# Expert 0 and overflow blocks in a leading loop, fifteen experts written out behind it, and the tables of two later layers built beside the second layer's output product

## The reference

```python
ang = positions[..., None] * inv_freq            # rope tables, same for both layers
cos, sin = jnp.cos(ang), jnp.sin(ang)
for l in range(2):
    q, k, v, cb, cc, cu, qm, gates = split(x @ w_in[l])
    q, k = rope(q, cos, sin), rope(k, cos, sin)
    lam = exp(sum(lq1[l] * lk1[l])) - exp(sum(lq2[l] * lk2[l])) + lam_init
    y_attn = diff_attention(q, k, v, lam, lam_init, g)
    y_mem = memory_attention_2(qm, mem, w_mem_kv[l])   # needs mem turned to columns
    x = layer_norm(ALPHA * x + merge(y_attn, conv, y_mem) @ w_out[l])
    x = layer_norm(ALPHA * x + grouped_moe(x, w_router, bias, w_gate[l], w_up[l], w_down[l]))
```

## Time and profile before

| | |
|---|---|
| median of 3 runs | 3729.55 us (3728.22 to 3733.88) |
| the profiled execution, its own time | 3737.84 us |
| its span in the trace | 3736.2 us |
| PE busy | 3048.7 us, 82% |
| DVE busy | 1926.2 us, 52% |
| ACT busy | 1078.1 us, 29% |
| DMA | 467.63 MB, mean 125 GB/s |
| mean granted TensorE clock | 0.889 of full |

### The profile page before, as it was taken

One profiled execution on the slowest core, in us unless ns is written; L12 is line 12 of the kernel. 1 busy time (PEld: TensorE's weight loads), 2 busy tenths in 40 slices (PEclk: granted clock), 3 DMA queues, 4 the chain that ended last, 5 costly groups with the idle time before them and its releaser, 6 DMA issues. The chain is left out here.

```text
span 3736.2 us, 35502 instructions
## 1 busy us (share of the span) xinstructions
PE 3048.7 (82%) x13366; PEld 2421.3 (65%) x13366; DVE 1926.2 (52%) x2791; ACT 1078.1 (29%) x1837; POOL 308.2 (8%) x472
## 2 busy tenths in 40 slices
PE   4969978798898498989985699749898998569973
PEld 3758856677776376766875477637676687457762
DVE  3562344351664444655543587644465454358754
ACT  2341130210441102151001477510215100147742
POOL 0020030000440001210000000010121000000001
PEclk8989999788899698979997799969997999779996
DMA  2212202122601131202323599623120222369973
GB/s 86 79 57 90 90 28 82 37 90 81 263 1 57 59 97 57 78 5 71 99 79 148 221 374 363 229 96 102 61 75 5 79 91 79 148 230 373 371 264 112
DMA packets 151663, 467.63 MB, mean 125 GB/s; under 512 B 15022, under 2 KB 29256, under 8 KB 126152
## 3 DMA queue, kind: packets, MB, share of 16 engines
q1 hardware_dynamic: 142136, 431.31, 32.6%
q0 software_dynamic: 9360, 34.08, 2.3%
HBM read 413.46 MB, written 51.90 MB: 125 GB/s over the span
## 5 line engine op out<-in xcount | busy, mean ns | idle before, releaser
L154 DVE CAST weights_r<-weights 128x1024 fp32r<-128x1024 f32 (+4 forms) x270 | 229.1, 848 | 845.1 <-DMA weights<-in_w_in 314.6
L147 PE MATMUL ps<-x_cols_hi_r,weights_r 128*128 128x512 f32 x896 | 361.9, 404 | 49.4 <-DVE weights_r L156 49.4
L156 DVE TENSOR_TENSOR weights_r<-weights,weights_r 128x1024 fp32r<-128x1024 f32 (+4 forms) x270 | 385.8, 1429 | 9.3
L148 PE MATMUL ps<-x_cols_lo_r,weights_r 128*128 128x512 f32 x896 | 357.9, 399 | 0.0
L149 PE MATMUL ps<-x_cols_hi_r,weights_r 128*128 128x512 f32 x896 | 357.9, 399 | 0.0
L147 PEld LDWEIGHTS ps<-x_cols_hi_r,weights_r 128*128 128x128 f32 x896 | 171.7, 192 | 95.6 <-DVE weights_r L156 54.1
L943 POOL TENSOR_SCALAR weights<-weights,weight 128x256 f32<-128x256 f32 (+3 forms) x304 | 152.5, 522 | 778.4 <-DVE weight L837 467.5
L887 ACT ACTIVATE weights<-weights,minus_top 128x256 f32<-128x256 f32 (+3 forms) x304 | 167.0, 551 | 147.3 <-DVE minus_top L800 147.3
L148 PEld LDWEIGHTS ps<-x_cols_lo_r,weights_r 128*128 128x128 f32 x896 | 171.6, 192 | 41.6 <-issue 1.4
L149 PEld LDWEIGHTS ps<-x_cols_hi_r,weights_r 128*128 128x128 f32 x896 | 171.3, 191 | 40.8
L147 PE MATMUL ps<-hawk_xT_hi_r,weights_r 128*128 128x512 f32 x384 | 155.5, 405 | 25.5 <-DVE weights_r L156 25.5
(11 more groups left out here) (466 smaller groups left out, 6947.2 us busy)
## 6 DMA issues: line engine op xcount, KB each, us to landing
weights<-in_w_in SPq DMA_DIRECT2D x64, 1024.0 KB, 5.3
raw_pieces<-in_w_exp_down SPq DMA_DIRECT2D x46, 1024.0 KB, 7.5
raw_pieces<-in_w_exp_up SPq DMA_DIRECT2D x36, 1024.0 KB, 7.1
weights<-in_w_exp_gate SPq DMA_DIRECT2D x34, 1024.0 KB, 6.1
raw_pieces<-in_w_exp_gate SPq DMA_DIRECT2D x32, 1024.0 KB, 6.3
weights<-in_w_exp_up SPq DMA_DIRECT2D x30, 1024.0 KB, 7.4
weights<-in_hawk_w_in SPq DMA_DIRECT2D x28, 1024.0 KB, 5.3
weights<-in_w_exp_down SPq DMA_DIRECT2D x20, 1024.0 KB, 8.0
```

What stands on the lines that cost most here:

```text
L147: pe.matmul(out, as_r(left[1]), as_r(right[0]), start=start, stop=False)
L148: pe.matmul(out, as_r(left[0]), as_r(right[1]), start=False, stop=False)
L154: dve.tensor_copy(as_r(hi), lo).then_inc(rounded, 1)
L156: dve.tensor_tensor(as_r(lo), lo, as_r(hi).bitcast(F32), ALU.subtract).then_inc(done, 1)
```

## The change

It has four parts.

1. `rope_tables`, `diff_lambda`, the rotation load and the turning of the second layers' memory are gone as stages. A "rider" (`tables_rider`) does their work inside the NSA output product: SP issues its twelve loads ahead of the weights, PE transposes the memory rows after steps 0 and 1 (into banks 4 to 7, which the left half does not use), ACT rounds them and does exponentials and sines, DVE works after the weight splits of steps 1 to 4. The results lie in tensors of the whole program; the attention memory tensors of the first layers use the same space.
2. `final_norm` is one stage, and norm and gain are one DVE pass.
3. In `experts` the loop stands first. Its iteration 0 is expert 0, the others are the overflow blocks; in each, SP loads the next block's x and pieces as the present block's are used, and DVE splits the down pieces ahead of `hidden`. After the last iteration the same rooms hold expert 1. Experts 1 to 15 are then written out. `route` computes the row slots for that order, with two more small loads and four more small DVE operations at its end.
4. In the written-out part the second up piece is rounded and split behind the hidden rows, not ahead of them.

The core of the diff (what is left out is the same code under new names, and the angle arithmetic, which is unchanged):

```diff
+    rider = rider or bag(names=(), sync=None, pe={}, dve={}, act=None)
+    with Tensors(nc) as sb, stage(nc, "weights_loaded*2", "rounded", "y_split", "weights_split", "read", *rider.names) as (block, s):
...
+            if rider.sync:
+                rider.sync(sp, s)
...
+                if q in rider.pe:
+                    rider.pe[q](pe, s)
...
                 if q == per_half:
                     add(0)
+                if q in rider.dve:
+                    rider.dve[q](dve, s)
...
+    def sync(sp, s):
+        sp.dma_start(rows[:, :, :], a["mem_2"][0].rearrange("(t p) d -> p t d", p=P)).then_inc(s.mem_loaded, 16)
+        sp.dma_start(pos[:, :], a["positions_2"].partition_broadcast(P)).then_inc(s.tables_loaded, 16)
+        sp.dma_start(freq[:, :], a["rope_freq"]).then_inc(s.tables_loaded, 16)
+        for i, name in enumerate(("q1", "q2", "k1", "k2")):
+            for layer in range(2):
+                sp.dma_start(lam[:, i, layer, :], a[f"lambda_{name}_2"][layer:layer + 1, :].partition_broadcast(P)).then_inc(s.tables_loaded, 16)
+        sp.dma_start(m.late.rotate[:, :], a["rotate"]).then_inc(s.tables_loaded, 16)
...
+    def turn(ks):
+        def run(pe, s):
+            pe.wait_ge(s.mem_loaded, 16)
+            for k in ks:
+                if k >= 4:
+                    pe.wait_ge(s.mem_split, k - 3)
+                for t in range(MT):
+                    mm = pe.transpose(m.ps[:, bank_of(k) + t * P:bank_of(k) + (t + 1) * P], rows[:, t, k * P:(k + 1) * P], m.ident[:, :])
+                mm.then_inc(s.mem_turned, 1)
...
+    def mem_low(ks):
+        def run(dve, s):
+            for k in ks:
+                dve.wait_ge(s.mem_taken, k + 1)
+                dve.tensor_tensor(as_r(memT.lo[:, k, :]), m.ps[:, bank_of(k):bank_of(k) + N_MEM], as_r(memT.hi[:, k, :]).bitcast(F32),
+                                  ALU.subtract).then_inc(s.mem_split, 1)
...
+    def lambdas(dve, s):
+        dve.wait_ge(s.tables_loaded, 16 * 11)
...
+               sync=sync, act=act, pe={0: turn(range(4)), 1: turn(range(4, DK)), 2: banks_free},
+               dve={1: both(mem_low(range(4)), lambdas), 2: mem_low(range(4, DK)), 3: angle(sin, 0.0),
+                    4: both(angle(cos, 0.25), finish_lambdas)})
...
+            for i in range(2):
+                sp.dma_start(own[:, i, :], a["own_block"][i:i + 1, :].partition_broadcast(P)).then_inc(s.loaded, 16)
...
+def ring_plan():
+    order = [(1, p) for p in GATE]
+    for b in range(1, N_EXPERTS):
         order += [(b, p) for p in UP]
...
+    room = {(1, p): p for p in range(6)}
+    room.update({(2, p): 6 + p for p in GATE + UP})
+    held = [job for job in order if job in room]
+    after = {}
+    for job in order:
+        if job not in room:
+            before = held.pop(0)
+            room[job], after[job] = room[before], order.index(before)
+            held.append(job)
...
+    for b, rooms in ((0, range(6)), (2, range(6, RAW_ROOMS))):
+        for room in rooms:
+            p = room % 6
+            sp.dma_start(as_loaded(raw[room], p), expert_piece(a, layer, b, p)).then_inc(m.expert_fetched, 16)
...
+            with sp.Fori(0, late) as i:
+                expert = sp.value_load(moe.late_expert[0:1, bass.ds(i, 1)], min_val=0, max_val=LAST)
+                row = sp.value_load(moe.late_row[0:1, bass.ds(i, 1)], min_val=0, max_val=MAX_BLOCKS - 1)
+                sp.wait_ge(s.first_x_turned, 2 * i + 2)
+                sp.dma_start(xe[:, :], rows_at(moe.x_rows, row)).then_inc(s.first_x_loaded, 16)
+                for p in range(6):
+                    sp.wait_ge(s.first_used, 6 * i + (7 + p))
+                    sp.dma_start(as_loaded(raw[p], p), expert_piece(a, layer, expert, p)).then_inc(s.first_loaded[p], 16)
...
+                sp.wait_ge(s.first_loaded[p], 16 * late + 16)
+                sp.sem_inc(s.loaded[p], 16)
...
+            with pe.Fori(0, late) as i:
+                pe.wait_ge(s.first_x_split, 2 * i + 2)
+                for p in GATE + UP:
+                    pe.wait_ge(s.first_split, 6 * i + (p + 1))
+                    project(xT[0], p, p, gate_bank if p in GATE else up_bank, s.first_used)
+                pe.wait_ge(s.first_x_loaded, 16 * i + 32)
+                turn_x(s.first_x_turned)
+                pe.wait_ge(s.first_hidden_done, i + 1)
+                turn_h(s.first_h_turned)
+                pe.wait_ge(s.first_h_split, i + 1)
+                pe.wait_ge(s.first_out_taken, 2 * i + 2)
+                for p in DOWN:
...
+                first_round(GATE + UP)
+                act.wait_ge(s.first_used, 6 * i + 8)
+                silu(s.first_silu_done)
+                first_round(DOWN)
+                act.wait_ge(s.first_used, 6 * i + 10)
+                act.wait_ge(s.first_h_turned, i + 1)
+                round_h(s.first_h_rounded)
+                round_x(xT[0], s.first_x_turned, 2 * i + 2, s.first_x_rounded)
+                act.wait_ge(s.first_used, 6 * i + 12)
+                act.wait_ge(s.first_y_left, i + 1)
+                take_out(s.first_out_taken)
...
+                if b > 1:
+                    static_take_out(b - 1)
+                if b < LAST:
+                    static_round_x(b + 1)
+                round_pieces(b, DOWN)
+                if b < LAST:
+                    round_pieces(b + 1, UP[:1])
...
+                if b < LAST:
+                    round_pieces(b + 1, UP[1:])
...
+                for p in GATE + UP + DOWN:
+                    dve.wait_ge(s.first_rounded, 6 * i + (p + 1))
+                    split_piece(p, p, s.first_split)
+                dve.wait_ge(s.first_silu_done, i + 1)
+                dve.wait_ge(s.first_used, 6 * i + 10)
+                hidden(s.first_hidden_done)
+                dve.wait_ge(s.first_h_rounded, i + 1)
+                split_h(s.first_h_split)
+                split_x(xT[0], s.first_x_rounded, 2 * i + 2, s.first_x_split)
...
+            for t in range(TT):
+                dve.scalar_tensor_tensor(out=x[:, t, :], in0=x[:, t, :], scalar=inv[:, t:t + 1], in1=g[:, :], op0=ALU.mult, op1=ALU.mult)
...
-        with stage(nc, "loaded") as (block, s):
-            @block.sync
-            def _(sp):
-                sp.dma_start(m.rotate[:, :], a["rotate"]).then_inc(s.loaded, 16)
-                sp.wait_ge(s.loaded, 16)
-        rope_tables(nc, m, a, cos, sin)
-        normed_memory(nc, m, a["mem_2"][0], None, memT)
```

646 lines of the change are left out of this document (319 added, 327 removed).

## The result

The changed kernel takes **3627.91 us** (median of 4 runs, 3617.87 to 3633.0) against 3728.89 for the kernel before (4 runs), a ratio of 0.9723 with a 95% interval of 0.9699 to 0.9747: 101 us less. The forecast was 3645.0 with a range from 3632 to 3670.

The account below looks back on a forecast made before the run. Bound: chain length between NSA product and next layer, PE in the product, PE with its wait in written-out blocks, DMA just behind. Terms summed to -84.6 us: 3737.84 to 3653.2, less 8.3 for the median, 3645.0; range 3632 to 3670.

Parts of the forecast that it names:

- Stages that go: Stages removed between NSA product and next layer (-31.5 and -0.9) and two lambda stages (-15.2); together -47.6 us.
- What the product takes on: NSA output product: 16 more PE transposes cost +2.1 us, DVE's added work fits its gaps; ends 1.5 and 14.
- 0 to 2: NSA output product: SP issues twelve loads ahead of the first weights' signal, costing 0 to 2 us.
- C: NSA output product: PE waits for DVE in steps 2 to 5; +14 instead of +2.1, 3656.9 us; chance 0.06.
- The loop: Expert loop: x rounding -1.0, table load +1.3, down wait -1.7, clock -1.5; -2.9 us each, three times -8.7.
- -8.7 - 2.8 + 1.2 + 1.6: Loop iterations, ramp into the written-out part, loop-count reads, and two more small router loads per layer, in us.
- The written-out blocks: Written-out experts: PE's hidden_T_lo wait goes, mean period 19.87 to 18.7 us, 26 times: -30.4; ends -15.6 and -38.
- rival B: Written-out blocks: HBM gives no more than 370 GB/s, the wait moves to a load; gain 0, 3675.4 us; chance 0.12.
- reserve: Written-out blocks: some 7.5 us of loads ahead, dry after 8.6 blocks at 18.4 us, then 19.27 us each.
- A: Written-out blocks: DMA binds from the first one, 19.27 us each; term -15.6, 3659.8 us; chance 0.20.
- E: Written-out blocks: ring never runs dry, 18.4 us throughout; term -38.2, 3637.2 us; chance 0.57 together with the forecast.
- D: Written-out blocks: lower clock makes down 2.7 us longer per block; +70, 3745.6 us; chance 0.02.

Follow-up runs that it names:

- e3: Changed kernel with `route` and `experts` of the kernel before, so only parts 1 and 2 are made; 3694.6 us (0.9900).
- e7_small: Changed kernel with four small costs taken out: rider loads issued later, own_block loads not awaited by PE, loop count read later, ACT's loop begun at silu; 3628.71 us.
- e5: Kernel before with part 3 alone, both up pieces still ahead of hidden_T_lo; 3732.02 us (1.0005).
- e2: Changed kernel with part 4 undone, both up pieces again rounded and split ahead of hidden_T_lo; 3677.71 us.
- e1: Kernel before with part 4 alone; 3683.04 us (0.9872).
- e4: Changed kernel with one of three matmul passes left out of the down product in the written-out blocks; 3586.1 us.
- e10: Changed kernel with one more 1 MB load, read by nobody, for each of blocks 2 to 14 of the written-out part; 3662.94 us.
- e9: e7_small with DVE following ACT's roundings of block 1 piece by piece, not waiting for all four; 3621.97 us (0.9709).
- e12: e9 with ACT rounding the next block's two gate pieces ahead of the outputs in the loop, and DVE splitting them there; 3598.32 us (0.9646).

## Why the prediction was right or wrong

**Stages that go: right.** Forecast -32.4 between product and next layer, measured -32.6 (44.76 to 12.18). PE starts 14.6 us behind the last add of the product, "some 15" in the forecast. The lambda stages: forecast -15.2; the stretch from projection to mask is 15.5 shorter in e3 and 18.4 in after, measured on the profiled execution of before. About 15 of it are the two stages (7.6 and 7.4 us in before); the rest is the scatter of the projection.

**What the product takes on: right mechanism, 1.5 short.** Forecast +2.1, measured +3.65. The transposes are 2.05 of it (PE's first 72 matmuls take 20.48 us with them, 18.43 without). 1.3 of the rest was the term set to "0 to 2" and counted as nothing: SP issues twelve loads ahead of the signal for the first weights, the last at 1151.40, and DVE begins on the weights 8.02 us into the stage, not 6.72:

```profile
1151.93 0.96 DVE L156 CAST weights_r<-weights 128x1536 fp32r<-128x1536 f32 x1 [3.06 <-SPq L186]
```

e7_small took this back (DVE begins 6.6 us into the stage). C (the angle work is not hidden) did not happen: PE's waits at the later weights are 0.61 and 0.26 us.

**The loop: right in size for an iteration, too much for the part.** Forecast -2.9 for each, measured -3.2 (34.05 to 30.83): x rounding, table load and shorter waits are all where they were said to be. But I counted a table load only between iterations. One also stands ahead of the first iteration's gate, where before had none, so PE's first gate comes 11.4 and 11.6 us behind the first load of x and not 10.1 and 10.2; and the stretch from the router's first load to that of the experts grew by 3.1 in both layers together, 0.3 more than forecast. Part 3 as a whole was forecast at -8.7 net (-8.7 - 2.8 + 1.2 + 1.6) and is worth -5.3 in its stages (e5, and e2 against e3).

**The written-out blocks: the failed step.** Forecast -30.4 (ends -15.6 and -38.2), measured -46.9 alone (e1) and 49.8 on undoing it (e2): beyond even the good end. Both floors were taken from busy times, and both were too high.

- "DMA has 0.97 x 19.87 = 19.27 us of work per block" took the share of busy time for an amount of work. Were it one, the share would have to grow with the rate, from 0.97 at 370 GB/s to 1.07 at 407; it is 1.01 there and still 1.01 at 421. The same bytes are counted as less busy time when they are asked for faster. Work would be bytes over the rate at the bound: 7.35 MB / 423 GB/s = 17.4 us, as e4 and e10 measured from two sides. The number was within reach: the earlier trace rows shows 429 GB/s in a stretch of loads alone, and I used it against rival B, but not for the floor of my own sum. By it the floor is 17.1, below PE, and no reserve runs dry. The Trainium skill says as much in its page "Perfetto Trace Analysis", section "Identifying the Most-Contended Engine": for DMA one should take the HBM utilization (which goes by bytes) and not the occupancy, since 16 engines make the occupancy misleading. This trace agrees, with the shares and rates just given.
- "PE alone would give 18.4" took PE's busy time with the wait in it. Matmuls overlap, and that overlap is lost at a wait. In the rows below the matmul ahead of the wait is busy for 0.39 us, where the next one would have started after 0.23, and the one behind the wait has its successor after 0.34 us and not 0.23. That is 0.16 + 0.11 = 0.27 us of busy time that goes with the wait: 18.37 - 0.27 = 18.10, and a wait of 1.5 us saved 1.77. Timeline of PE in the kernel before, one written-out block:

```profile
2297.44 0.39 PE L148 MATMUL ps<-raw_pieces_r,block_xT_hi_r 128*128 128x512 f32 x1
2297.67 0.39 PE L149 MATMUL ps<-x_cols_hi_r,block_xT_hi_r 128*128 128x512 f32 x1
2299.56 0.50 PE L147 MATMUL ps<-expert_hi_r,hidden_T_lo_r 128*128 128x512 f32 x1 [1.51 <-DVE hidden_T_lo_r L2411]
2299.90 0.39 PE L148 MATMUL ps<-weights_r,hidden_T_hi_r 128*128 128x512 f32 x1
```

Each of the two was worth 8 us: 26 x (18.7 - 18.4) for the DMA floor, 26 x (18.4 - 18.1) for PE's. That makes the 16 us by which this term fell short, and it is also the size of the miss of the whole. The other misses (1.5 us in the product, 3.4 in part 3) went the other way, and about as much came on top in stages that the change does not touch, which is luck.

Rivals A and B rested on the same share of 97% and fell with it: ACT never waits for a load in after, and the period is below 19.27 from the start. E, "the ring never runs dry", was the truth about the mechanism, and its price was 0.3 us a block too small. The rule of 358 GB/s that I weighed against this gain (the Trainium skill, "DMA: Bandwidth & Descriptors", section "Where 436 GB/s comes from") holds for two cores at once according to the Trainium skill's page "HBM Reference", section "Specifications (TRN2)", which gives some 425 GB/s to a core that streams alone. The 423 GB/s of e4 and e10, whose kernels run on one core, agree with that.

**The clock: right.** It is 1.00 in the written-out blocks (D did not happen). In the loop's down product it comes back after seven matmuls: 7.17 us against 8.5, forecast "half or a little more" of the 2.7; it was half.

**The range: too narrow for its reason.** Its low end took "18.4 throughout" for the best case. An end that comes from a busy time is not a bound. The time lies 4 us under that end.

## What to carry to other kernels

A share of busy time is no floor, neither for DMA nor for PE. For loads, divide the bytes by the best rate that any stretch of the same trace shows; for PE, take the matmuls by their spacing in a stretch without waits; and expect that the removal of a wait gives back a little more than its length (1.77 us for 1.5 here).

If a loop's iterations are far longer than the same work written out (30.8 against 18.1 us here), look at which engine idles at the iteration's end and let it begin the next one there. That was worth 24 us for three iterations, over four times what the loop part of the change brought. To shorten the gap without closing it gave next to nothing (e9), since the clock took back what the wait gave.

A signal that passes a count from one set of semaphores to another (e7) is a wait for everything that it counts. Pass it on piece by piece.

## What the runs showed of the hardware

- One core moves 421 to 423 GB/s over whole blocks when its transfers are the bound (loads but for 0.5 MB of 7.35), and 407 with a matmul stream at full clock beside them, with no wait on either side.
- The same stream of 992 matmuls at the same granted clock (0.97) takes 245.58, 246.44 or 247.37 us of busy PE, by kernel for the most part: 232.4, 233.3 or 234.3 ns from one to the next. Over a kernel of this size it makes some 9 us (estimate above), and its cause is open.
- The table loads in the loop depend here on where the loop stands and what it begins with. The loop of before, behind the written-out blocks, has none. In after, where it stands first, two run in each iteration, ahead of the first rounding and ahead of silu; in e7, e9 and e12, whose loop begins at silu, there is one, ahead of silu. A load takes 1.28 us, with nothing measurable around it (outputs end at 3249.36, the load begins at 3249.39, the rounding at 3250.68).
- A shorter gap is not always a gain: 1.4 us less of waiting in e9 came with a granted clock of 0.81 in place of 0.89 in the matmuls behind it, which took 1.1 us more.
